# A two-layer attention and expert-retrieval kernel: VectorE waits for its own steps by semaphore instead of draining, key numbers stay integers, one expert table per layer, softmax of the gates on ScalarE

## The reference, cut to what matters

```
def peer_ffn(x, w_q, sub_keys, u, v):
    q = (x @ w_q).reshape(B, S, 8, 2, 128)
    s = einsum('bshcd,cnd->bshcn', q, sub_keys)          # 2 x 128 key scores per head
    sv, si = top_k(s, 16)                                # 16 best of each half
    cand_s = sv[...,0,:,None] + sv[...,1,None,:]         # 256 pair sums
    cand_i = si[...,0,:,None] * 128 + si[...,1,None,:]   # expert number
    best_s, pos = top_k(cand_s, 16)
    e_idx = take_along_axis(cand_i, pos)
    gate = softmax(best_s)
    hid = gelu(einsum('td,ted->te', x, u[e_idx]))
    return einsum('te,ted->td', gate * hid, v[e_idx])
h = layer_norm(ALPHA*h + mix); h = layer_norm(ALPHA*h + peer_ffn(h))
```

## Time and profile before

| | |
|---|---|
| runs | 1515.42, 1516.98, 1517.38 us; median 1516.98 |
| profiled execution, span | 1518.3 us (the page gives no time for it outside the span) |
| PE busy | 1337.3 us, 88% |
| DVE busy | 1040.1 us, 69%, 2563 instructions |
| ACT busy | 690.4 us, 45% |
| gathers (queue q0) | 536.90 MB, 85.7% of the 16 DMA engines' span |
| all DMA | 597.98 MB, mean 394 GB/s |

### The profile page before, as it was taken

How to read it: one execution, slowest core, us unless ns; L and a number is a source line. 1 busy time by engine, 2 the same in 40 slices (tenths; PEclk the granted TensorE clock), 3 DMA queues, 4 the chain that set the end, 5 groups by cost and what they waited for, 6 DMA issues and landing times.

```text
span 1518.3 us, 16934 instructions
## 1 busy us (share of the span) xinstructions
PE 1337.3 (88%) x5068; PEld 724.6 (48%) x5068; DVE 1040.1 (69%) x2563; ACT 690.4 (45%) x2032; POOL 497.3 (33%) x527
## 2 busy tenths in 40 slices
PE   9999898987798888889999799899879998888786
PEld 8977554433354453445446645444335443333332
DVE  1137877778767777686654587777787767666655
ACT  2223554445544445436554244654554544444443
POOL 0003333334333333333320233343333333333331
PEclk9999999999999999999999999999999999999999
DMA  9749999999999999999989699999999999999996
GB/s 367 265 154 416 372 419 419 421 422 420 421 422 420 417 422 417 421 415 378 421 356 410 247 379 419 418 416 421 420 421 421 408 422 422 421 421 420 416 402 264
DMA packets 92398, 597.98 MB, mean 394 GB/s; under 512 B 10386, under 2 KB 13074, under 8 KB 26004
## 3 DMA queue, kind: packets, MB, share of 16 engines
q0 software_dynamic: 73728, 536.90, 85.7%
q1 hardware_dynamic: 18580, 60.01, 10.4%
HBM read 595.82 MB, written 1.05 MB: 393 GB/s over the span
## 4 chain that ended last, share of the span: by engine, by line
PE 33%; DMA 26%; DVE 24%; ACT 9%; issue 4%; DVEq 2%; POOL 1%; SPq 0%; another core or an unknown queue 0%; ACTq 0%; POOLq 0%
DMA uv<-in_peer_uv_dram,expert 26%; PE y L695 19%; DVE uv L1774 10%; PE y L541 3%; PE px L384 2%; PE y L409 2%; PE spare L582 2%; ACT L1321 2%; ACT diag L1329 2%; ACT wts L1323 1%; ACT L1279 1%; DVE key_idx L1619 1%; DVE hit L1611 1%; DVE key_idx L1613 1%; DVE pos L1641 1%
## 5 line engine op out<-in xcount | busy, mean ns | idle before, releaser
L695 PE MATMUL y<-uv,diag 128*128 128x512 f32 x1868 | 910.7, 622 | 154.3 <-ACT diag L1329 151.2
L1774 DVE CUSTOM_DVE_ANT_0 uv<-px,uv 128x1024 f32<-128x1024 f32 x512 | 616.8, 1221 | 296.7 <-DMA uv<-in_peer_uv_dram,expert 282.4
L1159 POOL DMA_INDIRECT uv<-in_peer_uv_dram,expert x512 | 491.8, 961 | 967.2 <-PE y L695 748.9
L695 PEld LDWEIGHTS y<-uv,diag 128*128 128x128 f32 x1868 | 337.1, 195 | 592.5 <-issue 299.7
L1321 ACT ACTIVATE act_hid<-hid 128x1 f32<-128x1 f32 x512 | 103.0, 201 | 590.1 <-DVE hid L1774 570.2
L1329 ACT ACTIVATE diag<-ident,wts 128x128 f32<-128x128 f32 x468 | 188.0, 402 | 43.9 <-ACT wts L1323 0.7
L1323 ACT ACTIVATE wts<-act_hid,gate 128x1 f32<-128x1 f32 x512 | 150.8, 294 | 16.6
L1321 ACT ACT_TABLE_LOAD x47 | 60.3, 1283 | 0.8
L1786 DVE SCALAR_TENSOR_TENSOR vsum<-uv,wts,vsum 128x1024 f32<-128x1024 f32 x41 | 52.7, 1284 | 10.0 <-ACT wts L1323 6.1
L1774 DVE DVE_READ_ACCUMULATOR2_ANT hid<- 128x1 f32 x512 | 42.5, 83 | 0.0
L1489 DVE TENSOR_TENSOR probs<-spare,bias 128x320 f32<-128x320 f32 x16 | 7.6, 474 | 44.9 <-PE spare L437 44.9
(11 more groups left out here) (312 smaller groups left out, 1292.3 us busy)
## 6 DMA issues: line engine op xcount, KB each, us to landing
uv<-in_peer_uv_dram,expert POOLq DMA_INDIRECT x512
uv<-in_na_w_dram SPq DMA_DIRECT2D x9, 512.0 KB, 8.7
w_q<-in_peer_w_q_dram SPq DMA_DIRECT2D x8, 512.0 KB, 12.7
uv<-in_mla_w_out_dram SPq DMA_DIRECT2D x8, 512.0 KB, 6.6
bias<-in_na_bias_dram SPq DMA_DIRECT2D x16, 160.0 KB, 6.9
w_vu<-in_na_w_dram SPq DMA_DIRECT2D x4, 512.0 KB, 8.8
w_latq<-in_na_w_out_dram SPq DMA_DIRECT2D x4, 512.0 KB, 6.1
latkv_room<-in_peer_w_q_dram SPq DMA_DIRECT2D x4, 512.0 KB, 11.8
```

Source lines behind the costliest of these rows:

```text
L695: last = T.matmul(Y[t][:, c, :], diag[:, acc_no(n) % DIAGS, :], uv[:, n % RING, 1, c * 512:(c + 1) * 512], start=False, stop=half_done)
L1159: pool.indirect_dma_start(uv[:, n % RING, :, :].rearrange("p h d -> p (h d)"), None, uv_table, bass.IndirectOffsetOnAxis(ap=expert[:, g % ...
L1774: V_.tensor_tensor_reduce(out=rows, in0=px[:, :, :], in1=rows, scale=1.0, scalar=0.0, op0=ALU.mult, op1=ALU.add, accum_out=hid[:, k:k + 1] ...
```

## The change

The change does the following.

- Nearly every `dve.drain()` goes. Where the next instruction reads the result of the one before, the producer increments a new semaphore `s_step` (or one it increments anyway) and the consumer waits for it. Four drains that stood between two steps that don't read each other's result at once have no such pair of their own: the one ahead of `add_on_vector` goes without a wait, and those ahead of `pair_top16`, at the start of `expert_numbers` (for groups after the first) and at the start of `join` become waits for a step that lies further back. One drain stays, the first of `rope_q`.
- The key numbers are no longer turned into floats (`key_numbers` goes, two instructions a group); the product of hits and numbers reads the integers; the sum gives two columns, and one fused instruction (first number times 128 plus second) replaces the cast to the expert number.
- The expert table comes as two inputs, one for each layer, so that the layer's offset is not added.
- The difference to the best score goes from DVE; ACT copies the negated best score and uses it as bias of the exponential, whose accumulator gives the sum. DVE keeps only the reciprocal. ACT multiplies the exponentials by it ahead of a group's first weight.
- In `first_choice` the first expert number is made directly after the eight best keys are indexed, ahead of the pair sums.

In all DVE has 784 instructions fewer, drains included.

```diff
-                dve.drain()
+                dve.wait_ge(s_step, steps[0])     # producers: ....then_inc(s_step, step())
...
-            uv_table = peer_uv.rearrange("l e d -> (l e) d")
             for layer in range(LAYERS):
+                uv_table = (peer_uv0, peer_uv1)[layer]
...
             def gate_exp(layer, g):
                 act.wait_ge(s_bd, layer * GROUPS + g + 1)
-                A.activation(best_e[:, :], best_d[:, :], ACT.Exp).then_inc(s_be, 1)
+                A.activation(neg_best[:, :], best[:, 0:1], ACT.Copy, scale=-1.0).then_inc(s_neg, 1)
+                act.wait_ge(s_neg, layer * GROUPS + g + 1)
+                A.activation(best_e[:, :], best[:, :], ACT.Exp, bias=neg_best[:, :], accum_out=gate_s[:, :]).then_inc(s_be, 1)
...
                 if k == 0:
                     act.wait_ge(s_gates, layer * GROUPS + g + 1)
+                    A.activation(gate[:, :], best_e[:, :], ACT.Copy, scale=gate_r[:, :])
...
-            def key_numbers(layer, some):
-                V_.tensor_scalar(key_idxf[:, 0, some], key_idx[:, 0, some], float(KEYS), float(layer * EXPERTS), ALU.mult, ALU.add)
-                V_.tensor_copy(key_idxf[:, 1, some], key_idx[:, 1, some])
...
-                V_.tensor_tensor(best_d[:, :], best[:, :], best[:, 0:1].broadcast_to([P, TOPK]), ALU.subtract)\
-                  .then_inc(s_bd, 1)
...
-                V_.tensor_tensor(hits, hits, key_idxf[:, :, 0:width].unsqueeze(1).broadcast_to([P, n, 2, width]), ALU.mult)
-                dve.drain()
-                V_.tensor_reduce(pick[:, some], hits.rearrange("p n c a -> p n (c a)"), X, ALU.add)
-                dve.drain()
-                V_.tensor_copy(expert[:, g % UNITS, chosen], pick[:, chosen]).then_inc(done, 1)
+                V_.tensor_tensor(hits, hits, key_idx[:, :, 0:width].unsqueeze(1).broadcast_to([P, n, 2, width]), ALU.mult)\
+                  .then_inc(s_step, step())
+                dve.wait_ge(s_step, steps[0])
+                V_.tensor_reduce(pick[:, some, :], hits, X, ALU.add).then_inc(s_step, step())
+                dve.wait_ge(s_step, steps[0])
+                V_.scalar_tensor_tensor(out=expert[:, g % UNITS, chosen], in0=pick[:, chosen, 0], scalar=float(KEYS),
+                                        in1=pick[:, chosen, 1], op0=ALU.mult, op1=ALU.add).then_inc(done, 1)
...
             def first_choice(layer):
...
+                dve.wait_ge(s_step, steps[0])
+                V_.scalar_tensor_tensor(out=expert[:, 0, 0:1], in0=key_idx[:, 0, 0:1], scalar=float(KEYS),
+                                        in1=key_idx[:, 1, 0:1], op0=ALU.mult, op1=ALU.add).then_inc(s_best, 1)
                 pair_sums(block.rearrange("p (a b) -> p a b", a=TOP), TOP)
-                dve.drain()
-                key_numbers(layer, slice(0, TOP))
-                V_.max(best[:, 0:8], block)
-                dve.drain()
-                V_.tensor_tensor(expert[:, 0, 0:1], key_idxf[:, 0, 0:1], key_idxf[:, 1, 0:1], ALU.add).then_inc(s_best, 1)
...
             def gates(layer, g):
                 dve.wait_ge(s_be, layer * GROUPS + g + 1)
-                V_.tensor_reduce(gate_s[:, :], best_e[:, :], X, ALU.add)
-                dve.drain()
-                V_.reciprocal(gate_r[:, :], gate_s[:, :])
-                dve.drain()
-                V_.tensor_scalar(gate[:, g % UNITS, :], best_e[:, :], gate_r[:, :], None, ALU.mult).then_inc(s_gates, 1)
+                V_.reciprocal(gate_r[:, :], gate_s[:, :]).then_inc(s_gates, 1)
...
             def add_on_vector(layer, g, k):
                 dve.wait_ge(s_wts, row_no(layer, g, k) + 1)
-                dve.drain()
```

More of the change, by code:

```diff
@@ L1477, in _, with step @@
                 V_.memset(Q_two[(1 - i) * HD:(2 - i) * HD, i, :], 0.0).then_inc(s_halves, 1)
+            steps = [0]
+            after = {}
+            def step():
+                steps[0] += 1
+                return 1
             def softmax_na(n):
@@ L1625, in pair_sums, with pair_top16 @@
+                after["keys", layer, g] = steps[0]
             def pair_sums(out, n):
                 V_.tensor_tensor(out, key_top[:, 0, 0:n].unsqueeze(2).broadcast_to([P, n, n]),
-                                 key_top[:, 1, 0:n].unsqueeze(1).broadcast_to([P, n, n]), ALU.add)
-            def pair_top16(layer):
+                                 key_top[:, 1, 0:n].unsqueeze(1).broadcast_to([P, n, n]), ALU.add).then_inc(s_step, step())
+            def pair_top16(layer, g):
+                dve.wait_ge(s_step, after["keys", layer, g])
@@ L1638, in pair_top16 @@
-                dve.drain()
-                V_.max(best[:, 8:16], cand_left[:, :])
-                dve.drain()
-                V_.max_index(pos[:, 8:16], best[:, 8:16], cand_left[:, :])
-                V_.tensor_tensor(best_d[:, :], best[:, :], best[:, 0:1].broadcast_to([P, TOPK]), ALU.subtract)\
-                  .then_inc(s_bd, 1)
-            def expert_numbers(g, some, width, skip, done):
+                V_.match_replace(cand_left[:, :], best[:, 0:8], flat, NEG).then_inc(s_step, step())
@@ L1646, in expert_numbers @@
+                dve.wait_ge(s_step, steps[0])
+                V_.max(best[:, 8:16], cand_left[:, :]).then_inc(s_step, step())
+                dve.wait_ge(s_step, steps[0])
+                V_.max_index(pos[:, 8:16], best[:, 8:16], cand_left[:, :]).then_inc(s_bd, 1)
+            def expert_numbers(layer, g, some, width, skip, done):
                 n = some.stop - some.start
                 hits = hit[:, 0:n * 2 * width].rearrange("p (n c a) -> p n c a", n=n, c=2)
-                dve.drain()
+                if width == TOPK:
+                    dve.wait_ge(s_bd, layer * GROUPS + g + 1)
+                else:
+                    dve.wait_ge(s_step, steps[0])
@@ L1750, in rope_q @@
                 V_.scalar_tensor_tensor(out=rope_b[:, :, :], in0=src[:, :, 1, :], scalar=MLA_SCALE,
-                                        in1=sin_t[:, where].unsqueeze(1).broadcast_to(shape), op0=ALU.mult, op1=ALU.mult)
-                dve.drain()
+                                        in1=sin_t[:, where].unsqueeze(1).broadcast_to(shape), op0=ALU.mult, op1=ALU.mult)\
+                  .then_inc(s_step, step())
+                dve.wait_ge(s_step, steps[0])
                 if t:
```

147 lines of the change are left out of this document (73 added, 74 removed).

## The result

Before 1516.84 us (median of 5, 1515.42 to 1517.38), after 1507.45 us (median of 5, 1506.48 to 1511.38): ratio 0.9947, 95% interval 0.9937 to 0.9958, some 8 us (6.4 to 9.6). The forecast was 1513.9, with 1511.2 as the lower end of its range: the sign was right, the size was not. Beside its rivals only R4 (more than the sum, 1511.5) lay on the right side, and it stayed 4 us short of what was measured. The profiled execution has a span of 1508.9 us, 1.5 above the median; the one of before stood as high above its own.

The account below looks back on a forecast made before the run. DMA gathers were taken to set the pace, so savings counted only where DMA falls short: place-by-place terms sum to 3.04 us, 1516.98 to 1513.9 us. Own range 1512.7 to 1515.0, 8-in-10 range 1511.2 to 1518.0.

Parts of the forecast that it names:

- R4: More than the sum: earlier diagonals avoid PE clock falls, 1.56 us in one or two places; about 1511.5 us, chance 0.12.
- What bounds the kernel: Gathers (DMA) set the pace in quiet steps; DVE savings count only where the DMA share falls below 1.
- The price of one edit: On DVE: 0.04 us saved per replaced drain, 0.17 per dropped one, 0.19 for key numbers; ACT's longer way costs 0.42.
- The sum, place by place: Savings added over the DMA holes, between the layers, first choice and tail: 3.04 us, giving 1513.9 us.
- Terms 1 and 5: First hole (156 to 164 us) and hole at 900 us: shorter expert choices, less ACT's 0.42, gain 0.96 and 0.76 us.
- Terms 2, 3 and 4: Hole near 690 us, one drain, 0.04; between the layers, ten drains, 0.40; layer 1's first choice, earlier first gather, 0.50.
- Term 6: Hole at 1454 us: replaced and dropped drains plus number edits 0.68, less ACT's 0.42, gain 0.26 us.
- Term 7: Tail: three drains behind the last matmul, gain 0.12 us.
- DVE work can't move it: Hole near 690 us: PE is busy 4.00 of 4.00 us there, so only one drain was credited, 0.04 us.
- R1: DVE's waits for its own semaphore cost what drains cost: 1.2 us gain remains, 1515.8 us, chance 0.24.
- R2: PE, the later engine, takes up DVE's gain in the first hole and at 900 us: 1516.0 us, chance 0.13.
- R3: Slower: ACT's longer way makes PE wait and its clock fall ahead of PE-bound stretches: 1521.9 us, chance 0.12.

Follow-up runs that it names:

- e18: Changed kernel plus six useless VectorE additions in each expert choice except those for groups 1, 2, 8 and 9 of each layer (53 us); 1507.66 us, ratio 0.9942.
- e14: Changed kernel plus three useless VectorE additions in each expert choice except those for groups 1, 2, 8 and 9 of each layer (26 us); 1509.89 us, ratio 0.9960.
- e17: Changed kernel plus six useless VectorE additions in each expert choice for groups 1, 2, 8 and 9 of each layer (19.2 us); 1517.18 us, ratio 1.0003.
- e2: Changed kernel with all drains back; integer key numbers, gates on ACT, two tables and early first number stay; 1516.74 us, ratio 0.9999 to the kernel before.
- e4: Kernel before with only the sum and product of the gates moved to ACT, drains and one table kept; 1516.98 us, ratio 1.0006.
- e3: Kernel before with only integer key numbers, the fused expert number and two tables, drains and gates kept; 1514.96 us, ratio 0.9993.

## Why the prediction was wrong, step by step

- *What bounds the kernel.* Right in the main: DMA sets the pace of the quiet steps. There are 51.9 us more of waiting in front of the dot products, and e18's 53 us cost 0.5 (but e14's 26 us cost 3).
- *The price of one edit.* Right to 0.01 or 0.02 us on DVE's own time line: 0.03 against 0.08 for a wait, 0.18 for a dropped drain, 0.20 for the key numbers, 0.41 on ACT; and 1.23 against 1.18 for a choice.
- *The sum, place by place*: this is **the step that failed**. It made 3.04 us where 8 to 9 were measured. Its core is 43 replaced drains on the path at 0.04 us, 1.7 us; e7, which has the replaced drains alone, measured 5.2 (3.3 to 7.0). So either more of them are on the path than it counted, or each one there carries more than its gap. By place:
  - *Terms 1 and 5* (first hole, hole at 900 us), 0.96 and 0.76, measured 1.5 (0.6) and 2.0 (1.4). At equal clock it is 1.1 and 0.7: as sums of DVE's and ACT's steps they were about right, and what they lacked goes with falls of the granted clock, which the prediction had set apart as R4.
  - *Terms 2, 3 and 4* (hole near 690 us, between the layers, first choice), 0.94 together, measured 3.3 (1.1) from 236 to 344 MB. This is the largest miss. e5, with waits in the choices alone, and e6, with the others alone, take 284.4 and 283.6 us there, against 284.1 like before and 280.9 like after: neither half gives the 3.3 by itself. Which wait does is open.
  - *Term 6* measured 0.9 (0.8) for 0.26. The quiet steps, priced at nothing, gave 0.5 (0.2) and 0.7 (0.6). *Term 7* measured 0.4 (0.5) for 0.12.
- *One choice per hole.* The eight choices of e17 are worth 8 times 1.23 times 0.52, about 5 us by the mean slope, where the forecast counted two of the eight, in terms 1 and 5. This is an estimate, with the falls of the clock inside it. e5, which has 0.96 of the 1.23 (no key numbers, no difference), would gain 4.0 by it and measured 3.5 (2.1 to 4.9).
- *"DVE work can't move it"*, on the hole near 690 us, is neither shown nor refuted: PE was busy 4.00 of 4.00 in e17's window too, and additions in the choice ahead changed nothing.
- *R1* (waits cost like drains) fell with e7, *R2* (the holes are filled otherwise) and *R3* (slower by the clock) with the result. *R4* was right in part: its mechanism is seen at two of the holes, and an estimate from the table of falls gives it 1.7 us, where it had 1.56 us in one or two places. It came to 1511.5 and not 1507.5 because the rest of its sum was the forecast's.
- *The parts priced near nothing* (two tables, gates on ACT, key numbers against ACT's longer way): nothing that can be told, by e2 to e4.
- *The chances*: the range ended at 1511.2, at R4 alone, and no rival said that the sum itself could be short by a factor of two or three.

Open: what gives the 3.3 us between 236 and 344 MB; why the choice for group 1 of layer 0 counts nearly in full (2.1 us for 2.4 at equal clock, one profile) and the one for group 2 not at all; and why e14 lost 3 us where e18 lost 0.5.

## What to carry to other kernels

A price per instruction can be right, and the sum still short by a factor of three, when the list of places where it counts is drawn from one trace. Three things helped here. Cut the execution by bytes moved, not by time, when two kernels move the same bytes; a window of fixed time showed a change near 690 us that other executions of like kernels show as scatter. Put known, useless work at the suspected places and at the others, at two doses, and then read in the trace at what time it ran: here half of it stood nowhere near the holes it was meant for. And compare executions in which the granted clock fell at a place with others in which it did too, before giving the difference to an edit. Where instructions depend on each other in a row, wait on a semaphore of one's own in place of a drain: on VectorE that alone was worth 8.2 us here (e1).

## What the hardware showed that was not expected

- A dependent VectorE instruction starts 0.03 us after its producer's end with a wait for the engine's own semaphore, 0.08 with a drain; an instruction that depends on nothing just before it starts, without either, together with the accumulator's read, 0.18 earlier than behind a drain.
- A DMA share of 1.00 need not mean the full throughput. Before, in the approach to the hole at 690 us, it stood at 383 GB/s, where the quiet stretch had 422. At 1204 to 1208 us, where part of the 0.7 us of layer 1's quiet steps arises, it was 1.00 at 377 GB/s before and 1.01 at 424 after:

```profile
680.00:684.00 4.00, 4.00 (x21) 2.80 (x22) 3.50 (x11) 0.50 (x2) 1.62 (x2) 1.00 1.00 383
```

- After one and the same idle time of 1.9 us the four matmuls of the first hole took 3.03 us in one execution of the changed kernel and 1.98 in another; after 1.66 and 1.67 us the eight ahead of the hole at 900 us took 5.40 us in the kernel before and 3.70 in e3.
